# Branch A's projection and the first half's output by seven block products instead of eight

## What is computed

```python
h = rmsnorm(x, g_pre)
q_a,k_a,v_a,lr_a,z_a,q_b,k_b,v_b,z_b,m_a,m_b = split(h @ w_in)
o_a = rmsnorm(gla(q_a,k_a,v_a,decay(lr_a)), g_gla) * silu(z_a)   # branch A
o_b = sliding_window_attention(rope(q_b),rope(k_b),v_b,sinks) * silu(z_b)  # branch B
y   = sigmoid(m_a + b_a) * (o_a @ w_branch_gla) + sigmoid(m_b + b_b) * (o_b @ w_branch_swa)
out = x + rmsnorm(y @ w_out, g_post)
```

## Time and profile before

| what | value |
| --- | --- |
| median of three runs | 1955.2 us |
| profiled execution: time, span | 1951.45 us, 1949.6 us |
| TensorE matmuls (PE) | busy 1911.5 us, 98% of the span |
| VectorE (DVE) | 1239.7 us, 64% |
| ScalarE (ACT) | 844.6 us, 43% |
| GpSimd (POOL) | 987.4 us, 51% |
| DMA | 359.42 MB, mean 184 GB/s |

### The profile page before, as it was taken

How to read it: one execution, slowest core, us unless ns; L and a number is a source line. 1 busy time by engine, 2 the same in 40 slices (tenths; PEclk the granted TensorE clock), 3 DMA queues, 4 the chain that set the end, 5 groups by cost and what they waited for, 6 DMA issues and landing times. The chain is left out here.

```text
span 1949.6 us, 28906 instructions
## 1 busy us (share of the span) xinstructions
PE 1911.5 (98%) x9972; PEld 1533.0 (79%) x9972; DVE 1239.7 (64%) x2069; ACT 844.6 (43%) x1893; POOL 987.4 (51%) x667
## 2 busy tenths in 40 slices
PE   8999999999999999999999999999999999999996
PEld 7878877777777777888888787877777777788885
DVE  6868876977776667623154888768577675763104
ACT  5466474543444443324333664544433444432221
POOL 4643455555433357643563445557654333775444
PEclk9999999999999999999999999999999999999998
DMA  7524375667667677745433334457767666775612
GB/s 277 157 73 135 107 243 185 198 216 228 203 193 238 214 241 254 237 140 197 138 120 108 102 115 162 154 182 241 229 192 233 214 220 218 275 249 162 196 42 87
DMA packets 255140, 359.42 MB, mean 184 GB/s; under 512 B 31059, under 2 KB 156563, under 8 KB 242195
## 3 DMA queue, kind: packets, MB, share of 16 engines
q1 hardware_dynamic: 254995, 357.57, 56.9%
HBM read 237.50 MB, written 120.00 MB: 183 GB/s over the span
## 5 line engine op out<-in xcount | busy, mean ns | idle before, releaser
L878 PE MATMUL pu<-a_hi,w_hi 128*128 128x512 f32 x1740 | 688.8, 398 | 10.3 <-DVE u L1769 6.4
L878 PE MATMUL pu<-a_hi,w_lo 128*128 128x512 f32 x1740 | 674.6, 390 | 0.5 <-POOL w_lo L1888 0.5
L878 PE MATMUL pu<-a_lo,w_hi 128*128 128x512 f32 x1740 | 673.7, 390 | 0.0
L1888 POOL TENSOR_TENSOR w_lo<-t,w_hi 128x512 fp32r<-128x512 f32 x244 | 347.7, 1431 | 402.7 <-ACT w_hi L1222 402.6
L1888 POOL TENSOR_TENSOR w_lo<-w_raw,w_hi 128x512 fp32r<-128x512 f32 x267 | 378.9, 1429 | 254.5 <-ACT w_hi L1222 254.5
L878 PEld LDWEIGHTS pu<-a_hi,w_hi 128*128 128x128 f32 x1740 | 326.5, 188 | 94.2 <-issue 26.3
L878 PEld LDWEIGHTS pu<-a_hi,w_lo 128*128 128x128 f32 x1740 | 326.6, 188 | 70.6 <-POOL w_lo L1888 0.9
L878 PEld LDWEIGHTS pu<-a_lo,w_hi 128*128 128x128 f32 x1740 | 327.0, 188 | 63.6
L879 PE MATMUL pu<-a_hi,w_hi 128*128 128x512 f32 x640 | 249.2, 389 | 0.0
L879 PE MATMUL pu<-a_lo,w_hi 128*128 128x512 f32 x640 | 249.0, 389 | 0.0
L879 PE MATMUL pu<-a_hi,w_lo 128*128 128x512 f32 x640 | 249.0, 389 | 0.0
(11 more groups left out here) (183 smaller groups left out, 2476.3 us busy)
## 6 DMA issues: line engine op xcount, KB each, us to landing
w_raw<-in_w SPq DMA_DIRECT2D x81, 1024.0 KB, 7.0
va_d<-ct SPq DMA_DIRECT2D x32, 256.0 KB
qb_d<-ct SPq DMA_DIRECT2D x32, 256.0 KB
zb_d<-ct SPq DMA_DIRECT2D x32, 256.0 KB
q_s<-qb_d SPq DMA_DIRECT2D x32, 256.0 KB, 3.8
z_s<-zb_d SPq DMA_DIRECT2D x32, 256.0 KB, 3.1
gb_d<-gb SPq DMA_DIRECT2D x32, 256.0 KB, 3.6
za_d<-ct SPq DMA_DIRECT2D x32, 256.0 KB
```

What stands on the lines that cost most here:

```text
L878: return nc.tensor.matmul(dst, weights, moving, start=start, stop=stop, skip_group_check=True)
L1888: TT(flat(w_lo[o.n % NWB][:, :, :]), src, as_f32(flat(w_hi[o.n % NWB][:, :, :])), ALU.subtract) \
```

## The change

The order of groups becomes: h, yB, yA of half 0; h, yB, yA of half 1; out of half 0; out of half 1. Every phase but the last opens with one plain group and goes on with three (or 28) fast ones. In particular:

- yA 1 to 3 of both halves and out 1 to 3 of half 0 are fast; group 0 of `h` in half 1 becomes plain. 595 slots become 587.
- Every phase has the fill table of yB, with S1 to S4 (not the last, which has A11 to A22 alone). `split_late` on VectorE goes.
- y (the result of yA) is stored to `y_d` and loaded as fills; L1436 and L1931 go.
- Row sums: jobs `SumJob` for gb (as before), for ga at slots 4, 10, 16, 22 after yB's start (into a second set of `gx`), for y of half 0 at r = 84, 94, 104, 114 of half 1. A job's four TTs lie in two steps, two in each.
- `gate_a` and `yb` have four buffers each; loads for yA j + 1 are issued once tile n of yA j is done, one group ahead.
- The sixteen tiles of half 0 are normalized during the last phase, at slots 9 to 24 of its 32, one a slot, both operations on VectorE, with seven buffers. Their rstd is made at its slots 3 to 6.
- Column sums T1 to T4 stay on VectorE for every fast group (`col_sum_on_vector` returns True, now with the name as argument).

```diff
-for _sb in range(NSB):
-    for _n, (_kind, _idx) in enumerate(ORDER):
-        _fast = (_n < NH and not (_sb == 0 and _n < PLAIN)) or (_kind == "yB" and _idx > 0)
+for _sb, _ws in ((0, range(NH + 8)), (1, range(NH + 8)), (0, range(NH + 8, NH + 12)), (1, range(NH + 8, NH + 12))):
+    for _w in _ws:
+        _kind, _idx = ORDER[_w]
+        _plain = _w in (0, NH, NH + 4, NH + 8) or (_sb == 0 and _w < PLAIN) or (_sb == 1 and _kind == "out")
...
-    for _name, _load, _split, _free in (("A11", 19, 23, 22), ("A12", 20, 24, 23), ("A21", 24, 27, 24),
-                                        ("A22", 25, 28, 25)):
-        fill(_sb, "ga", _name, GA_SLOT[_sb][_name], _e + _load, _e + _split, _e + _free)
-    if _sb + 1 < NSB:
...
+for _sb, _what in PHASES:
+    _e = first_slot(_sb, dict(gb="yB", ga="yA", h="v", y="out")[_what])
     for _name, _load, _split, _free in (("A11", -10, -6, -7), ("A12", -9, -5, -6), ("A21", -5, -2, -5),
                                         ("A22", -4, -1, -4), ("S2", -1, 2, -3), ("S1", 0, 3, -2), ("S3", 3, 7, 6),
                                         ("S4", 4, 9, -1)):
...
-NORM = {99 + 3 * x: x for x in range(16)}
-GPREP = {152 + 10 * j: j for j in range(KH)}
-NORM_BUFS = 3
+SUMS = 3
+RB_END = 6
+NORM = {9 + x: x for x in range(16)}
...
+for _sb in range(NSB):
+    _jobs = [("gb", BASE[0] + 152 + 10 * j, 0) for j in range(KH)]
+    if _sb:
+        _jobs = [("y", BASE[1] + 82 + 10 * j, 0) for j in range(KH)] + [("gb", BASE[1] + 150 + 10 * j, 0)
+                                                                        for j in range(KH)]
+    _jobs += [("ga", YBASE[_sb] + 4 + 6 * j, 1) for j in range(KH)]
...
+            def load_sums(job):
...
+                    elif job.what == "ga":
+                        sp.wait_ge(ga_out, 16 * 16 * (job.sb + 1))
...
+                sp.wait_ge(gs_out, 16 * 4 * job.n)
+                for q in range(4):
...
+                    go(gx[job.place][q][:, :], rows_d[job.what][e * P:(e + 1) * P, t0:t0 + HT], gx_in)
...
+                for job in SUM_JOBS:
+                    if s == job.first + 2:
+                        store_sums(job)
+                    if s == job.first - 3:
+                        load_sums(job)
...
+                for job in SUM_JOBS:
+                    for k in ((0, 1), (2, 3))[s - job.first] if s - job.first in (0, 1) else ():
+                        dve.wait_ge(gx_in, 16 * 4 * (job.n + 1))
+                        dve.wait_ge(gs_ok, 4 * job.n + k)
...
+                    if g and g.kind == "yA" and g.fast:
+                        n = fast_no(g)
+                        dve.wait_ge(gate_a_in[tile_n], 32 * (4 * g.sb + g.idx + 1))
+                        if tile_n:
+                            dve.wait_ge(c_ok[tile_n], n + 1)
+                            STT(ct[tile_n][:, :], gate_a[tile_n][:, :], 1.0, ct[tile_n][:, :], ALU.add, ALU.mult) \
+                                .then_inc(yg_ok, 1)
...
+                        TT(ct[tile_n][:, :], ct[tile_n][:, :], yb[tile_n][:, :], ALU.add).then_inc(f_ok[tile_n], 1)
-                if s - 1 in SPLIT_AT and low_on_vector(SPLIT_AT[s - 1]):
-                    split_late(SPLIT_AT[s - 1])
```

More of the change, by code:

```diff
@@ L66 @@
 ROPED = ("kvB", "qB")
[L67 to L69 removed]
+STORED = [g.n for g in GROUPS if not (g.kind == "out" and g.sb == NSB - 1)]
+FINISHED = [g.n for g in GROUPS if g.fast and g.kind not in ("qk", "v", "out")]
+FINISHED_0 = [g.n for g in GROUPS if g.kind in ROPED or (g.kind == "yA" and g.fast)]
 def upto(groups, n):
@@ L162, with jobs_done @@
 HPREP = {100 + 12 * j: j for j in range(KH)}
-NORM = {99 + 3 * x: x for x in range(16)}
-GPREP = {152 + 10 * j: j for j in range(KH)}
-NORM_BUFS = 3
+SUMS = 3
+RB_END = 6
+NORM = {9 + x: x for x in range(16)}
+SumJob = namedtuple("SumJob", "n sb what j first place")
+SUM_JOBS = []
+for _sb in range(NSB):
[4 more added lines that the diff above has]
+    _jobs += [("ga", YBASE[_sb] + 4 + 6 * j, 1) for j in range(KH)]
+    for _k, (_what, _first, _place) in enumerate(_jobs):
+        SUM_JOBS.append(SumJob(len(SUM_JOBS), 0 if _what == "y" else _sb, _what, _k % KH, _first, _place))
+def jobs_done(sb, what):
+    return max(j.n for j in SUM_JOBS if (j.sb, j.what) == (sb, what)) + 1
+NORM_BUFS = 7
 WARM = (32, 12)
@@ L180, in rel @@
     sb = 1 if s >= BASE[1] else 0
[L181 to L186 removed]
+    return sb, s - BASE[sb] + sb * (PLAIN - 1)
 def two_pi_parts(n):
@@ L1925, in _ @@
                 for c in range(4):
-                    g = step(s, 2 * c + 2)
-                    if g and g.kind == "yA":
-                        number = 16 * g.sb + 4 * g.idx + c
-                        pool.wait_ge(y_hi_ok, number + 1)
-                        place = Y_SLOT[g.sb][QUARTERS[c]]
-                        TT(a_lo[place][:, g.idx, :], ct[c][:, :], as_f32(a_hi[place][:, g.idx, :]), ALU.subtract) \
-                            .then_inc(y_lo_ok, 1)
                     g = step(s, 2 * c + 1)
-                    if g and g.kind == "out" and 2 * g.idx + c % 2:
+                    if g and g.kind == "out" and not g.fast and 2 * g.idx + c % 2:
                         number = 4 * g.idx + c
@@ L1939, in _ @@
                         half = c // 2
-                        pool.wait_ge(out_ok, 16 * g.sb + number + 1)
+                        pool.wait_ge(out_ok, 4 * g.sb + number + 1)
                         pool.wait_ge(acc_ok, 14 * g.sb + adds)
-                        TT(acc[half][:, :], acc[half][:, :], tmp[c % 2][:, :], ALU.add).then_inc(acc_ok, 1)
+                        TT(acc[g.sb][half][:, :], acc[g.sb][half][:, :], tmp[c % 2][:, :], ALU.add).then_inc(acc_ok, 1)
+                for k, n in enumerate(TILE_ORDER):
+                    g = step(s, 5 + k)
+                    if g and g.kind == "out" and g.fast:
+                        number = 4 * (g.idx - 1) + k
+                        pool.wait_ge(sq_out_ok, number + 1)
+                        pool.wait_ge(acc_ok, 2 + number)
+                        TT(acc[0][n // 2][:, :], acc[0][n // 2][:, :], tmp[k % 2][:, :], ALU.add).then_inc(acc_ok, 1)
                 if r - 2 in SWA:
```

446 lines of the change are left out of this document (227 added, 219 removed).

## The result

The changed kernel takes 1999.9 us, the median of 4 runs (1996.8 to 2005.3), beside 1954.5 for the kernel before on the same chip: a ratio of 1.023, interval 1.0202 to 1.0259. It is slower. The profiled execution took 1996.81 us (span 1994.9), 45.4 more than the 1951.45 of before. Forecast were 1953.0, range 1940 to 1967: the time is far outside.

The account below looks back on a forecast made before the run. TensorE, busy 98% of the span, was taken as the bound. Terms -22.4 + 7 + 0.5 + 10 + 1 + 1.5 + 0.5 = -1.9 us gave 1949.5 profiled, median 1953, range 1940 to 1967.

Parts of the forecast that it names:

- Products: Whole kernel: 595 products become 587, 8 x 2.72 = 21.8 us off.
- The jobs in yB: Branch A's row sums made during yB groups 1 to 3: 10 us added in all, 3 to 20.
- branch A's group 1 near 23 us: Sign to look for in the profile: yA group 1 at about 23 us, against 19.04 for its products.
- Branch A, groups 2 and 3: Fast groups after branch A's opening: work covered by the products, 0.5 us for both halves, 0 to 3.
- the opening's term: Branch A group 1, after the plain group: engine turns add 7 us for both halves, 3.5 to 12.
- Output of half 0: Output group 1 of the first half, squares added on GpSimd: 1.5 us added, 0 to 4.
- h in half 1: Second half's h group 1, S3 and S4 split on GpSimd: 1 us, 0 to 2.3; old 0.58 us stall goes.
- The last phase: Final 32 products take the first half's sixteen normalized tiles: covered, nothing if SP is under 6 products late.
- The chain of jobs on SP: Rival, yB groups 1 to 3: jobs' load and store cycle of 20.1 us sets the pace; 1966, chance 0.26.
- The full gain: Rival: loads land early, plain groups absorb turns, openings cost what yB's does now; about -15 us, 1940, chance 0.17.
- The end grows: Rival, last phase: SP reaches the sixteen tiles so late that the last gating waits; about 1957, chance 0.04.
- the attention's: Second half's attention stage, 16 TTs for the output's sums replacing the normalized tiles: 0.5 us, -0.5 to 3.

Follow-up runs that it names:

- the repairs: Changed kernel plus last phase's small work later, two sum jobs before yB, third job's loads 6 products ahead, one yB store a product earlier: 1975.3 us.
- the first case: Changed kernel with branch A's jobs keeping all additions, but only the first job's loads and no stores: 1989.1 us, one run.

## Why the prediction was wrong

*Products* (-21.8): right.

*The jobs in yB* (+10, ends 3 and 20): the largest miss, 15 us in yB and most of the 14.4 in branch A's plain group; 30 in all. Two steps of it failed. It charged four additions by turns as 2.7 us, their own 0.68 each. Where VectorE and GpSimd alternated one for one, an addition came every 1.70 us, and the partial sums queued behind had to wait for all of it; and eight additions, not four, were in group 1's way, since the first job's ran 3.3 us into it. The turn was rightly named and wrongly priced, by its length and by its number. And the SP lateness was costed as 1.2 us a cycle inside yB only. The step that a moved queue must be followed to its end was not done: the stores of yB's last group, of which the one shown is 3.5 us later than without jobs, are waited for by branch A's plain group (TensorE 5.0 us, where it is 1.7 without). The forecast's own sign for it, branch A's group 1 near 23 us, was looked for one group too late: that group took 20.5 and 19.5, and the 7th product of the group ahead had the stall.

*The granted clock* is missing from the sum. Before, none of its stalls moved it: the slices showed it full but at the end, and each stall was priced at its own length. After, the four longest gaps of yB and branch A (4.8 to 7.6 us between matmuls) were each followed by 7 to 12 matmuls at the lower level, and of the five of 2.4 to 3.2 us in the whole trace in which nothing else ran on TensorE two by 7 and three by none. Of the 67.2 us, 11.6 are this.

*Branch A, groups 2 and 3* (+0.5): 3.4. "Covered" was worked out as a mean over the group. Its stalls are at its first and fourth product (0.7 and 1.2 us, in nearly every kernel): the work of a group is not spread evenly over it. Together with groups 0 and 1 this branch cost 19.7 over its products for the 7.5 forecast; without jobs 12.5 were left (2.0, 2.2, 1.9 and 2.2, 2.3, 1.9): 8.7 in groups 0 and 1, for which the opening's term had 7 (3.5 to 12), and 3.8 in group 2, over the 3 at the high end of its own. So the opening itself was a little mis-sized and what follows it more.

*Output of half 0* (+1.5, ends 0 and 4): 6.3, of which 5.3 in group 1, where GpSimd was busy for all of its 24.4 us with the additions of squares on top, and TensorE waited 2.03 us for `u`, with some slow matmuls after it (clock 0.93 over the stage). The direction was seen. Its slack in the plain group ahead wasn't there: that one has 1 us of excess itself. Which of the additions is to blame was not tried.

*h in half 1* (+1, and 0.6 of an old stall off): 1.6 net, which looks right and isn't. Of the 2.7 us that its first two groups had over the products before, 1.8 were small matmuls of the first half's sums of squares, which went to the last phase. The stalls there are 4.4 us now (1.23 before the 7th product of the plain group, 2.00 for `u` in the next, the rest in small steps), over the high end of 2.3: two errors that cancel by luck.

*The last phase* ("covered, nothing"): +13.5. The step named the sixteen tiles and their cover, and this cover held. It overlooked that the sums of squares and their small matmuls move with them, to product 3 and 6, when GpSimd still makes `a_lo` of the fills. 9.7 us were this queue, shown by moving them to 6 and 9; 3.7 is their own length, and stood in h before. VectorE's 81 idle us said nothing of GpSimd's order.

*The rivals.* The chain of jobs on SP (1966) had the place, and half of the mechanism: it is what branch A's plain group waits for. It didn't have the turns, by which yB group 1 is long even with no more than one job's loads. The rate by which it was also argued, 357 GB/s, isn't what decides: 355 flow in the same stage without jobs too, where it takes 6 us less. Nor is it a ceiling here; with the jobs, 416 flowed for 7 us of that stage:

```profile
837.50:844.70 7.20, 5.30 (x13) 4.17 (x14) 6.07 (x5) 2.50 (x5) 6.64 (x4) 0.57 1.04 416
```

The full gain (1940) is excluded: without jobs yB's opening costs 2.7 and 2.5 us, but h's 6 us, the output's 7 and branch A's 12.5 in two halves. The end grows (1957) was named for the wrong reason, a late SP.

*How the errors combined.* The sum of all high ends was +21.9. Measured were +45.4, since every term but the products and the attention's went over its own high end (h's by its stalls), and the clock had none. With the repairs added one after the other the kernel went from 1999.9 to 1975.3, while the stages that were repaired fell by 9.7, about 22, 9.3 and 12.5 us. So more than half of what was removed came back elsewhere: at the next wait, and 4 to 5 us ahead of yB.

## What to carry to other kernels

Leaving out products is worth their length only while the engines that feed them have slack product by product, not in the mean of a group: before a saving is added up, write down for each product what stands ahead of its first operand on VectorE, GpSimd and the DMA-issuing queue, and price every operation that shares a turn at the length of the turn (1.70 us here, not 0.68). Follow a delayed queue until something is issued on time again, and everything that moves with a moved step to the engine that makes its input. And where TensorE has run at full clock, a stall can cost more than its length: here each of those over 4 us did.

## What was not expected of the hardware

Four additions on VectorE beside additions on GpSimd take 6.50 and 6.60 us, 1.63 to 1.65 each, against 0.68 alone, and in the first case only the first job had loads, landed by then. The Trainium skill, page "SBUF — State Buffer", section "Who interferes with whom", calls the port pair that VectorE and GpSimd share an exclusive lock, and says that a VectorE instruction with two SBUF inputs contends with a GpSimd one that reads SBUF. The trace agrees: the two alternated, and each pair took 1.70 us from start to start, where the lengths alone, 0.68 and 1.29, make 1.97.

The granted clock went to 0.50 in the 6.7 us in which TensorE waited, and the next 12 matmuls ran at that level, 2.4 us more than at the full one (12 x 0.2). Filling the gaps with matmuls nobody reads removed 31 of the 58 slow starts and gained nothing (2006.8 us against 1999.9).
